# Squares summed over k by TensorE from pairs, modulation chunks in runs of four behind each quarter's first part, gate bursts of two, one and two

## The chip, the cores and the metric

The kernel runs on one core of a Trainium2 chip. The metric is the time of one execution on the device in microseconds (us). The engines are TensorE (PE), VectorE (DVE), ScalarE (ACT), GpSimd (POOL) and SyncE (SP); SP issues nearly all transfers, and its instructions, like those of every engine, run in the order in which they are written.

## The reference

One layer of a hybrid diffusion backbone is applied to 128 context tokens and 512 latent tokens with 2,048 channels, all in fp32. What matters here is its beginning:

```python
shift, scale, gate = jnp.split(mod, 3, axis=-1)   # mod = silu(c) @ w_ada + b_ada, once for c_ctx and once for c
h = rms_norm(x, norm_w)                            # x * rsqrt(mean(x*x) + EPS) * norm_w
h = h * (1.0 + scale[:, None, :]) + shift[:, None, :]
proj = h @ w_in                                    # 2048 -> 9216: nine parts of eight heads
...
out = jnp.concatenate([o_r, o_h], axis=-1).astype(x.dtype) @ w_out
x = x + (gate[:, None, :] * out).astype(x.dtype)
```

Between `proj` and `out` stand multi-scale retention and the HGRN2 recurrence, per head and in both directions. The final normalisation follows.

## The kernel before

**Tiles.** x lies transposed, as 16 tiles of 128 channels by 640 tokens (`x_in[:, k, :]`, k from 0 to 15; the first 128 columns are context tokens, the other 512 latent). A projection product takes fp32 operands that were split into a high and a low part in a reduced format (`w_hi`, `w_lo`, `hT_hi`, `hT_lo`) and computes hi*hi, hi*lo and lo*hi, each over two halves of 320 tokens: six products for each k. A chunk of w_in is 128 x 1024 values, eight k of 128 output columns; 18 chunks make a head. ACT writes `w_hi`, DVE writes `w_lo` (`split`), in two buffers, from three landing buffers (`raw`).

**Start.** Four loads bring x. ACT squares the 16 tiles into a ring of four buffers (`x_squares`, which borrows the place of the constants from column NSTART on). DVE adds them one after another into `var`. After the first modulation chunk PE multiplies `var` with a matrix of ones, which sums over the partitions (two products, L1726 and L1727), DVE and ACT make the reciprocal root, and DVE goes on with the modulation.

**Quarters.** The modulation vector is a product of `cs` (the two silu vectors) and w_ada. It is loaded in chunks of 1,024 KB (`load_ada`, tile `ada_raw`, four slots; `in_w_mod` chunks 0 to 31, then five of `in_w_first`); PE takes each with 16 fp32 products of 32 output rows (`ada_chunk`). Four chunks are a group; groups 0 to 3 give the scale of a quarter of the channels (four k). Behind a group PE transposes its row (`modulation_columns`), DVE scales x by it (L1096), ACT writes `hT_hi`, DVE `hT_lo` (L1102). Then `ahead(s)` can use these four k: for six slices of head 0, three "ahead" parts s of 24 products for each quarter. The loop over `group` from 1 to 4 is written out in the order below; PE runs it in just this order. A chunk's slot is free when PE has used it, and only then SP issues the load four chunks on. Into SP's list of modulation loads are put the first 12 w_in chunks and, at chunk 12, three small loads.

```python
ahead(s0)
ada_chunk(c0)
ada_chunk(c0 + 1)
ahead(s0 + 1, range(0, 2))
ada_chunk(c0 + 2)
ada_chunk(c0 + 3)
ahead(s0 + 1, range(2, 3))
modulation_columns(group)
ahead(s0 + 1, range(3, 4))
ahead(s0 + 2)
```

**Head 0 behind it.** Chunks 6 to 9 take the other modulation chunks between their products, and at the end five correction chunks (`correction`), which account for the shift. Chunks 10 to 17 are token chunks: five tiles of 128 tokens, each with six products of 512 columns. Between these tiles PE multiplies the gate's weights: 32 pieces of 512 KB (`gate_half`, `in_w_gate`, four slots, which are two of the modulation's slots), GATE_EACH of them behind tile number `at` in the chunk's order. `load_gate` waits until PE has used the piece four before. SP's `items(n, ...)` of head 0 hold, in order, the constants (n = 7), gate loads (n = 11 on), the retention states (n = 6) and eight copies that swap rows of the rotated keys and queries (n = 12, `swapped`), each from a wait of its own; w_in chunks from 12 on are loaded in between. Heads 1 to 7 follow, then the output projection.

## Time and profile before

| | |
|---|---|
| median of 3 runs | 1,489.37 us (1,489.04 to 1,490.95) |
| profiled execution, its time | 1,491.68 us |
| profiled execution, its span | 1,489.9 us |
| PE busy | 1,436.9 us, 96% of the span |
| DVE, ACT, POOL busy | 60%, 33%, 25% |
| chain that ended last: PE | 90% |
| chain that ended last: DMA, DVE | 4%, 3% |

The table is to be read with care at one place: a share over the whole span hides stages with different limits. PE's idle time is what the chain can lose, and the rows below show where it lies, by stage.

### The profile page before, as it was taken

The page shows a single profiled execution, that of the slowest core. Times are in us where ns is not written, and L with a number is a line of the kernel's source. Part 1 is how long each engine was busy: PE and PEld are TensorE (multiplying, and loading weights), DVE is VectorE, ACT ScalarE, POOL GpSimd, SP SyncE. Part 2 cuts the span into 40 slices and gives each one's busy share as a digit, 9 for nine tenths or more (in the row PEclk, how much of TensorE's full clock was granted, in tenths as well). Part 3 has the DMA queues.
Part 4 walks back from the last instruction along what each step waited for, and adds up shares of the span by engine and source line. Part 5 has one row for each costly group of instructions (what it writes and reads, how often), then busy time and mean ns, then how long its engine had stood idle before and what let it go on. Part 6 is the DMA issues. An engine that isn't in the chain of part 4 may idle for free.

```text
span 1489.9 us, 28075 instructions
## 1 busy us (share of the span) xinstructions
PE 1436.9 (96%) x11678; PEld 1278.6 (86%) x11678; DVE 889.0 (60%) x1208; ACT 493.5 (33%) x851; POOL 373.6 (25%) x292
## 2 busy tenths in 40 slices
PE   2999899999999999999999999999999999999996
PEld 2899569988998899889988998999899988788884
DVE  6634766565666665666576556666675658632346
ACT  4222334333333333333323332333243234321234
POOL 0000011532052216221621261135114415301220
PEclk9999999999999999999999999999999999999998
DMA  9789972322231223222313131322223237264236
GB/s 379 279 324 394 333 263 95 107 72 87 70 107 58 93 75 96 75 89 65 107 61 106 47 121 47 106 84 85 91 78 92 73 130 246 75 214 149 85 116 223
DMA packets 68763, 201.01 MB, mean 135 GB/s; under 512 B 8224, under 2 KB 16672, under 8 KB 62768
## 3 DMA queue, kind: packets, MB, share of 16 engines
q1 hardware_dynamic: 68656, 199.38, 38.7%
q8 instruction: 92, 1.51, 0.4%
q14 instruction: 15, 0.12, 0.0%
HBM read 178.62 MB, written 16.53 MB: 131 GB/s over the span
## 4 chain that ended last, share of the span: by engine, by line
PE 90%; DMA 4%; DVE 3%; SPq 1%; ACT 1%; POOL 0%; issue 0%; DVEq 0%; ACTq 0%
PE ps L1801 35%; PE ps L1830 10%; PE ps L1832 9%; PE ps L1831 9%; PE ps L2010 4%; PE ps L2012 4%; PE ps L2011 4%; PE ps L1853 2%; DMA area<-in_w_mod 2%; PE ps L1696 2%; PE ps L1717 2%; DMA area<-in_w_gate 1%; PE ps L1781 1%; PE ps L1866 1%; DVE area L1096 1%; DMA area<-in_w_out 1%
## 5 line engine op out<-in xcount | busy, mean ns | idle before, releaser
L1055 DVE TENSOR_TENSOR w_lo<-area,w_hi 128x1024 fp32r<-128x1024 f32 x144 | 184.4, 1280 | 374.7 <-ACT w_hi L621 374.2
L621 ACT ACTIVATE w_hi<-area 128x1024 fp32r<-128x1024 f32 x144 | 152.4, 1059 | 565.2 <-PE ps L1832 270.7
L1801 PE MATMUL ps<-hT_hi,w_hi 128*128 128x320 f32 x1184 | 276.8, 315 | 0.0
L1801 PE MATMUL ps<-hT_lo,w_hi 128*128 128x320 f32 x1184 | 269.7, 309 | 0.0
L1801 PE MATMUL ps<-hT_hi,w_lo 128*128 128x320 f32 x1184 | 269.7, 309 | 0.0
L1830 PE MATMUL ps<-w_hi,hT_hi 128*128 128x512 f32 x640 | 255.0, 398 | 0.0
L1832 PE MATMUL ps<-w_hi,hT_lo 128*128 128x512 f32 x640 | 249.6, 390 | 0.0
L1831 PE MATMUL ps<-w_lo,hT_hi 128*128 128x512 f32 x640 | 249.4, 390 | 0.0
L1801 PEld LDWEIGHTS ps<-hT_hi,w_hi 128*128 128x128 f32 x1184 | 195.7, 188 | 3.7 <-issue 1.4
L1801 PEld LDWEIGHTS ps<-hT_lo,w_hi 128*128 128x128 f32 x1184 | 198.0, 188 | 0.0
L1801 PEld LDWEIGHTS ps<-hT_hi,w_lo 128*128 128x128 f32 x1184 | 197.9, 188 | 0.0
L1830 PEld LDWEIGHTS ps<-w_hi,hT_hi 128*128 128x128 f32 x640 | 120.2, 188 | 28.5 <-issue 4.7
L1832 PEld LDWEIGHTS ps<-w_hi,hT_lo 128*128 128x128 f32 x640 | 120.1, 188 | 25.7
L1831 PEld LDWEIGHTS ps<-w_lo,hT_hi 128*128 128x128 f32 x640 | 120.3, 188 | 23.4
L1158 DVE RECIPROCAL area<-area 128x320 f32<-128x320 f32 x64 | 134.5, 2131 | 1.3
L2010 PE MATMUL ps<-w_hi,hT_hi 128*128 128x512 f32 x320 | 126.5, 395 | 2.2 <-DVE w_lo L1439 2.0
L2012 PE MATMUL ps<-w_hi,hT_lo 128*128 128x512 f32 x320 | 124.7, 390 | 0.0
L2011 PE MATMUL ps<-w_lo,hT_hi 128*128 128x512 f32 x320 | 124.7, 390 | 0.0
L1439 DVE TENSOR_TENSOR w_lo<-area,w_hi 128x1024 fp32r<-128x1024 f32 x40 | 53.2, 1330 | 111.9 <-ACT w_hi L899 111.9
L1617 POOL TENSOR_TENSOR area<-area 128x320 f32<-128x320 f32 x56 | 80.4, 1436 | 156.6 <-ACT area L746 156.6
L1606 POOL TENSOR_TENSOR area<-area 128x320 f32<-128x320 f32 x56 | 41.5, 741 | 301.6 <-PE ps L1853 244.8
L746 ACT ACTIVATE area<-area 128x1280 f32<-128x1280 f32 x56 | 71.3, 1273 | 122.1 <-DVE area L1254 117.4
(248 smaller groups left out, 1898.7 us busy)
## 6 DMA issues: line engine op xcount, KB each, us to landing
area<-in_w_in SPq DMA_DIRECT2D x144, 512.0 KB, 3.5
area<-in_w_mod SPq DMA_DIRECT2D x32, 1024.0 KB, 8.9
area<-in_w_out SPq DMA_DIRECT2D x40, 512.0 KB, 3.7
area<-in_w_gate SPq DMA_DIRECT2D x32, 512.0 KB, 5.8
area<-in_x_columns SPq DMA_DIRECT2D x4, 1280.0 KB, 9.9
area<-in_w_first SPq DMA_DIRECT2D x5, 1024.0 KB, 7.8
o_hi_scratch<-area SPq DMA_DIRECT2D x14, 320.0 KB, 2.2
o_lo_scratch<-area SPq DMA_DIRECT2D x14, 320.0 KB, 2.6
```

The lines of the kernel that those rows point to most:

```text
L621: act.activation(w_hi[:, n % 2, :], raw[:, n % 3, :], ACT.Copy).then_inc(wt_hi.sem, 1)
L746: act.activation(x, x, ACT.Exp).then_inc(xe.sem, 1)
L1055: v.tensor_tensor(w_lo[:, n % 2, :], raw[:, n % 3, :], w_hi[:, n % 2, :].bitcast(F32), ALU.subtract).then_inc(wt_lo.sem, 1)
L1158: v.reciprocal(part, part).then_inc(signal.sem, 1)
L1617: g.tensor_tensor(x[:, :, left], x[:, :, left], kf[:, :, left], ALU.mult)
L1801: ins = mm(out[s], wt[:, n % 2, w], x[:, k, s * HALF:(s + 1) * HALF], start=k == 0 and step == 0, stop=k == KT - 1 and step == 2)
L1830: mm(out, hT_hi[:, k, tile_cols(t)], w_hi[:, n % 2, w], start=k == 0, stop=False)
L1831: mm(out, hT_hi[:, k, tile_cols(t)], w_lo[:, n % 2, w], start=False, stop=False)
L1832: i = mm(out, hT_lo[:, k, tile_cols(t)], w_hi[:, n % 2, w], start=False, stop=k == KT - 1)
L2010: mm(out, hT_hi[:, k, tile_cols(t)], w_hi[:, m % 2, w], start=k == 0, stop=False)
L2011: mm(out, hT_hi[:, k, tile_cols(t)], w_lo[:, m % 2, w], start=False, stop=False)
L2012: return mm(out, hT_lo[:, k, tile_cols(t)], w_hi[:, m % 2, w], start=False, stop=k == KT - 1)
```

## The change

Four things are changed. (1) DVE adds the squares only in pairs, in place, and PE sums the eight pairs into two banks with eight pairs of products, ahead of the first modulation chunk; ACT waits for `x_total` before it writes a buffer again. (2) In the quarters the four modulation chunks of a group follow each other behind `ahead(s0)`; in the first group one chunk stands behind each of the first two k. The transposition comes behind the first k of the next part. Split 2 moves behind its quarter's last k. (3) The constants are loaded behind modulation chunk 16. (4) The gate pieces are taken two, one and two behind tiles 0, 2 and 4 of a token chunk (before: two behind tile 1, three behind tile 4), and their loads are written behind the other items of SP, up to three pieces further.

```diff
-GATE_FIRST, GATE_EACH = 10, (2, 3)
+GATE_FIRST, GATE_EACH = 10, (2, 0, 1, 0, 2)
...
             def items(n, h, prev):
-                if n == UNITS + 1 and prev is None:
-                    sp.wait_ge(x_sum.sem, x_sum.at(KT - 2))
-                    sp.dma_start(con[:, NSTART:NCONST], consts[:, NSTART:NCONST]).then_inc(con_in.sem, 16)
-                if prev is None and n > GATE_FIRST:
-                    for k in range(GATE_SLOTS, 6) if n == 11 else range(5 * n - 54, min(5 * n - 49, GATE_HALVES)):
-                        load_gate(k)
...
+            def gate_loads(n):
+
+                for k in range(max(5 * n - 51, GATE_SLOTS), min(5 * n - 46, GATE_HALVES)) if n > GATE_FIRST else range(0):
+                    load_gate(k)
+
             def head(h, prev):
                 for n in range(CHUNKS):
                     if not first_head(h) or n >= 12:
                         load(h, n)
                     items(n, h, prev)
+                    if prev is None:
+                        gate_loads(n)
...
+                if c_ == 16:
+                    sp.wait_ge(x_total.sem, x_total.at(KT // 2 - 1))
+                    sp.dma_start(con[:, NSTART:NCONST], consts[:, NSTART:NCONST]).then_inc(con_in.sem, 16)
...
-                if k >= SQUARES:
-                    act.wait_ge(x_sum.sem, x_sum.at(max(k - SQUARES - 1, 0)))
+                if k >= SQUARES and k % 2 == 0:
+                    act.wait_ge(x_total.sem, x_total.at((k - SQUARES) // 2))
                 act.activation(x_squares[:, k % SQUARES, :], x_in[:, k, :], ACT.Square).then_inc(x_sq.sem, 1)
...
-            for k in range(1, KT):
-                dve.wait_ge(x_sq.sem, x_sq.at(k))
-                if k > 1:
-                    dve.wait_ge(x_sum.sem, x_sum.at(k - 2))
-                v.tensor_tensor(var, x_squares[:, 0, :] if k == 1 else var, x_squares[:, k % SQUARES, :], ALU.add).then_inc(x_sum.sem, 1)
+            for j in range(KT // 2):
+                one, two = (x_squares[:, (2 * j + i) % SQUARES, :] for i in range(2))
+                dve.wait_ge(x_sq.sem, x_sq.at(2 * j + 1))
+                v.tensor_tensor(one, one, two, ALU.add).then_inc(x_sum.sem, 1)
...
+            for j in range(KT // 2):
+                pair = x_squares[:, 2 * j % SQUARES, :]
+                pe.wait_ge(x_sum.sem, x_sum.at(j))
+                mm(ps[:, A, :], ones, pair[:, P:T], start=j == 0, stop=j == KT // 2 - 1)
+                mm(ps[:, BB, 0:P], ones, pair[:, 0:P], start=j == 0, stop=j == KT // 2 - 1).then_inc(x_total.sem, 1)
...
             for group in range(1, QUARTERS + 1):
                 c0, s0 = group * GROUP_CHUNKS, (group - 1) * AHEAD
...
+                if group == 1:
+                    for k in range(ADA_K):
+                        ahead(s0, range(k, k + 1))
+                        if k < 2:
+                            ada_chunk(c0 + k)
+                else:
+                    ahead(s0)
+                for c_ in range(c0 + 2 if group == 1 else c0, c0 + GROUP_CHUNKS):
+                    ada_chunk(c_)
+                ahead(s0 + 1, range(0, 1))
                 modulation_columns(group)
-                ahead(s0 + 1, range(3, 4))
+                ahead(s0 + 1, range(1, 4))
                 ahead(s0 + 2)
```

**PE in the first token chunk, chunk 10.** Before: the products of the second tile (the last three of them), the five small correction transposes (L1761), the first two gate pieces (L1781), the third tile.

```order
L1830 MATMUL ps<-w_hi,hT_hi 128x512
L1831 MATMUL ps<-w_lo,hT_hi 128x512
L1832 MATMUL ps<-w_hi,hT_lo 128x512
L1761 MATMUL ps<-con,area 128x32 [waits corr_rows]
L1761 MATMUL ps<-con,area 128x32 x4
L1781 MATMUL ps<-area 32x256 [waits g_landed0]
L1781 MATMUL ps<-area 32x256 x3
L1781 MATMUL ps<-area 32x256 [waits g_landed1]
L1781 MATMUL ps<-area 32x256 x3
L1830 MATMUL ps<-w_hi,hT_hi 128x512 [waits corr_rows]
```

Of the change, from the end of the first tile (L1786 are the gate pieces, L1766 the transposes):

```order
L1835 MATMUL ps<-w_hi,hT_hi 128x512
L1836 MATMUL ps<-w_lo,hT_hi 128x512
L1837 MATMUL ps<-w_hi,hT_lo 128x512
L1786 MATMUL ps<-area 32x256 [waits g_landed0]
L1786 MATMUL ps<-area 32x256 x3
L1786 MATMUL ps<-area 32x256 [waits g_landed1]
L1786 MATMUL ps<-area 32x256 x3
L1835 MATMUL ps<-w_hi,hT_hi 128x512
L1836 MATMUL ps<-w_lo,hT_hi 128x512
L1837 MATMUL ps<-w_hi,hT_lo 128x512
```

The first two pieces have moved ahead of one tile, and the transposes now stand one tile behind them.

**SP at the gate loads.** Before, behind the last correction chunks (L404); L508 are small bias rows, L456 the retention states, L440 the constants, L473 the swaps:

```order
L412 DMA area<-in_w_gate 128x1024 [waits a_used] x4
L508 DMA area<-in_b_ada 2x512 [waits g_clear]
L508 DMA area<-in_b_ada 2x512 x3
L456 DMA area<-in_state_ret_fwd 128x128 [waits h_lo]
L456 DMA area<-in_state_ret_bwd 128x128
L440 DMA con<-in_constants 128x2688 [waits x_sum]
L412 DMA area<-in_w_gate 128x1024 [waits g_used] x2
L429 DMA area<-in_w_in 128x1024 [waits wt_lo]
L412 DMA area<-in_w_gate 128x1024 [waits g_used] x5
L473 DMA area<-area 32x512 [waits r_fixed]
L473 DMA area<-area 32x512 x7
L429 DMA area<-in_w_in 128x1024 [waits wt_lo]
```

Of the change (L450 the states, L467 the swaps):

```order
L450 DMA area<-in_state_ret_fwd 128x128 [waits h_lo]
L450 DMA area<-in_state_ret_bwd 128x128
L412 DMA area<-in_w_gate 128x1024 [waits g_used] x5
L429 DMA area<-in_w_in 128x1024 [waits wt_lo]
L467 DMA area<-area 32x512 [waits r_fixed]
L467 DMA area<-area 32x512 x7
L412 DMA area<-in_w_gate 128x1024 [waits g_used] x5
L429 DMA area<-in_w_in 128x1024 [waits wt_lo]
```

The constants are gone from here, five gate loads now stand ahead of the w_in load and of the swaps, and the next five stand behind the swaps.

**ACT at the squares.** Before, the second four squares wait once each for the running sum:

```order
L611 ACTIVATE con<-area 128x640 [waits x_landed0] x4
L611 ACTIVATE con<-area 128x640 [waits x_sum,x_landed1] x4
L611 ACTIVATE con<-area 128x640 [waits x_sum,x_landed2] x4
L611 ACTIVATE con<-area 128x640 [waits x_sum,x_landed3] x4
L621 ACTIVATE w_hi<-area 128x1024 [waits landed0]
```

Of the change:

```order
L615 ACTIVATE con<-area 128x640 [waits x_landed0] x4
L615 ACTIVATE con<-area 128x640 [waits x_total,x_landed1]
L615 ACTIVATE con<-area 128x640 [waits x_landed1]
L615 ACTIVATE con<-area 128x640 [waits x_total,x_landed1]
L615 ACTIVATE con<-area 128x640 [waits x_landed1]
L615 ACTIVATE con<-area 128x640 [waits x_total,x_landed2]
```

Every second square now waits for a product of PE instead of an addition of DVE.

## Rows read from the trace of the kernel before

**Rows 1.** Busy time by stage: window, us, each engine, granted clock, DMA, GB/s.

```profile
0.00:35.61 35.61, 8.33 (x134) 5.93 (x134) 22.48 (x40) 15.87 (x23) 0.73 (x5) 0.98 0.94 379
35.61:101.62 66.01, 62.96 (x806) 58.61 (x807) 35.00 (x68) 16.82 (x21) 0.00 (x0) 0.96 0.78 310
101.62:148.15 46.53, 45.94 (x741) 42.53 (x739) 16.47 (x43) 9.84 (x16) 0.00 (x0) 1.00 0.92 368
148.15:215.68 67.53, 61.70 (x449) 41.81 (x446) 47.02 (x69) 22.76 (x36) 5.08 (x4) 1.00 0.88 316
215.68:1489.90 1274.22, 1257.95 (x9560) 1129.68 (x9558) 768.05 (x989) 428.20 (x755) 367.83 (x283) 1.00 0.31 101
```

**Rows 2.** Timeline of the start: start us, duration us, engine, instruction, idle before.

```profile
7.79 2.61 ACT L611 ACTIVATE con<-area 128x640 f32<-128x640 f32 x4 [4.51 <-DMA area<-in_x_columns]
9.19 0.82 DVE L1050 TENSOR_TENSOR area<-con 128x640 f32<-128x640 f32 x1 [4.78 <-ACT con L611]
...
17.55 2.62 ACT L611 ACTIVATE con<-area 128x640 f32<-128x640 f32 x4 [0.48 <-DMA area<-in_x_columns]
...
23.29 2.08 PE L1726 MATMUL ps<-area,con 128*128 128x512 f32 x2
...
25.16 0.64 PE L1727 MATMUL ps<-area,con 128*128 128x128 f32 x2
...
25.83 0.69 DVE L1060 TENSOR_SCALAR area<-ps 128x512 f32<-128x512 f32 x1 [1.67 <-PE ps L1727]
...
31.47 0.29 DVE L1076 COPY area<-ps 128x128 f32<-128x128 f32 x1
```

**Rows 3.** Timeline of PE, two fp32 products of head 0's successor.

```profile
246.53 0.38 PE L1877 MATMUL ps<-area 128*128 128x128 f32 x2
246.75 0.39 PE L1878 MATMUL ps<-area 128*128 128x128 f32 x2
```

**Rows 4.** Chain of work that ended last, 35 to 102 us: start, duration, what.

```profile
35.61 6.12 PE ps L1717 x24
...
58.44 1.88 PE ps L1696 x64
...
65.77 13.57 DMA area<-in_w_mod
...
97.22 4.40 PE ps L1717 x30
```

**Rows 5.** Waits, 0 to 350 us: total us, times, longest.

```profile
PE ps L1717 <- DVE hT_lo L1102: 6.0, 4, 3.5
```

**Rows 6.** Timeline of PE at the second quarter's products.

```profile
56.40 0.57 PE L1717 MATMUL ps<-hT_hi,w_hi 128*128 128x320 f32 x2 [1.60 <-DVE hT_lo L1102]
```

**Rows 7.** Busy time by window: three short stretches.

```profile
34.00:35.00 1.00, 0.00 (x0) 0.00 (x0) 1.00 (x3) 0.81 (x2) 0.00 (x0) 0.50 1.00 418
56.00:60.00 4.00, 3.60 (x72) 3.41 (x76) 1.54 (x3) 1.44 (x2) 0.00 (x0) 1.00 0.01 2
65.00:68.00 3.00, 3.00 (x23) 3.00 (x22) 2.54 (x9) 0.84 (x2) 0.00 (x0) 1.00 0.15 50
```

**Rows 8.** Timeline of PE at gate pieces of the first token chunks.

```profile
161.19 0.64 PE L1781 MATMUL ps<-area 128*32 128x256 f32 x8 [2.57 <-DMA area<-in_w_gate]
...
164.70 1.12 PE L1781 MATMUL ps<-area 128*32 128x256 f32 x16
...
170.06 1.50 PE L1781 MATMUL ps<-area 128*32 128x256 f32 x24
171.50 0.50 PE L1830 MATMUL ps<-w_hi,hT_hi 128*128 128x512 f32 x1
```

**Rows 9.** Timeline of PE's weight loads at the second gate piece.

```profile
152.67 0.16 PEld L1781 LDWEIGHTS ps<-area 128*32 128x32 f32 x8 [0.38 <-DMA area<-in_w_gate]
```

**Rows 10.** Timeline of SP's issues at the constants and the swaps.

```profile
150.26 0.56 SPq L440 DMA_DIRECT2D con<-in_constants  x1
...
166.26 5.07 SPq L473 DMA_DIRECT2D area<-area  x8
```

29 lines of the change are left out of this document (8 added, 21 removed).

## The prediction

> **What bounds the kernel now.** I read first the busy time by stage [rows 1]. TensorE (PE) is busy for 1,257.95 of the last 1,274.22 us, and the change touches nothing there. What it can win lies before 215.68 us: PE idles 27.3 us until the first projection product at 35.61, 3.05 us in the four quarters until 101.62, 0.59 us until 148.15, and 5.83 us in the six token chunks until 215.68, 36.8 us together. The DMA share beside it is 0.94, 0.78, 0.92 and 0.88, so that the transfers are nearly as tight as PE: a PE wait that goes away may come back at the next transfer. Then I read each stage's own limit.
>
> Start: the squares of x on ScalarE (ACT) follow four loads of x, which come 3.25 us apart (7.79 to 17.55), VectorE (DVE) adds one tile after another from 9.19 to 23.0, two fp32 products on PE give the sum at 25.80, and the DVE chain of the variance, Newton step and first modulation copy begins at 25.83 and reaches the copy at 31.47 [rows 2]. The reader is to see that 5.64 us distance; the change does not touch it. Quarters: the chain runs through PE, through the DVE conversions behind each modulation, and through one transfer, the modulation chunk that is issued at 65.77 and lands 13.57 us later [rows 4]; PE waits for the conversions four times, 6.0 us in all, of which 3.5 is the first [rows 5] and the longest other 1.6 [rows 6]. Of the 3.05 us the three later ones are 2.5, which leaves 0.5 for the wait for that chunk. Token chunks: three waits for gate pieces, 2.57 us in the first chunk; they sum to the 5.83 us of that stage [rows 1, 8].
>
> **The squares.** Fifteen adds become eight, and one pair of products becomes eight pairs. DVE loses 7 x 0.85 us, which was on the path, but ACT now waits, before every second square from the fifth on, until PE has summed the pair whose buffers it overwrites: two pairs in flight. One turn of that ring is ACT 1.4 us for two squares (2.61 for four, and the end of the second), DVE 0.85, and PE. At the lower clock level PE needs 2.5 us for a pair (23.29 to 25.80 [rows 2]); at the higher, 128-column fp32 products start 0.22 us apart [rows 3], so 640 columns take 1.1 us and the result 0.2 more. The turn is 1.4 + 0.85 + 1.3 and three hand-overs of 0.04, 3.65 us for two pairs. The first pair is ready at 9.19 + 0.85 = 10.0 and summed at 12.6. PE starts slow: 24 products from 35.61 took 6.12 us where 30 took 4.40 later [rows 4], so the higher rate came some 5 us after PE began; the granted clock there is 0.50, the lower level of 1.2 GHz [rows 7]. Counted from 10.0 this is 15. The odd pairs are then summed at about 14.6, 18.3, 21.9 and 25.6, the even ones earlier. If the rate rises at 13.5 the last is at 25.4, at 17 it is 26.2. I take 25.8, as before: the term is 0, bounds -0.4 and +0.4. The serial adds have been exchanged for a ring with the same end. The cover of the four modulation chunks that now come behind the sums is the DVE chain: they take 3.8 us (two take 1.88 [rows 4]) where 5.64 is free; without it they would stand on the path with 3.8.
>
> The Trainium skill (TensorE: Matmul & The Clock Gate, the HAM clock gate) says that an array that has been idle starts at its lower rate and that sustained work releases it. By that rule alone the gaps in the new ring could keep it low; the rows do not show products with such gaps, and the rival for it is below.
>
> **The quarters.** A product takes 4.40/30 = 0.147 us, a modulation chunk 0.94, a switch between the two kinds 0.1. In the first group one chunk stands behind each of the first two k, which costs two switches (0.2) and brings the group's transposition from 48.4 to about 46.8: twelve products (1.76) now stand behind it instead of before it. In each later group the run of four saves two switches. Behind the transposition PE has 42 products, 6.17 us, instead of 30, 4.40. The 1.77 us more cover the longest of the three later waits for conversions, 1.6, in which split 2 stood, and so all 2.5 us of them go [rows 5, 6]; if that cover were gone, they would be back. Split 2, moved behind the quarter's last k, is done some 4 us before its product.
>
> What comes late next is the transfer. Group 2's chunks run from 56.6, so the load for group 3's first chunk is issued at 57.6; it was 59.5, behind the chunk at 58.44 [rows 4]. The DMA queue is empty before (0.01 busy from 56 to 60) and crawls behind the three small loads (0.15 busy from 65 to 68 [rows 7]); both move along with it. The fourth chunk then lands at 79.34 - 1.9 = 77.4. Between the third's landing and it stand a w_in and itself, 512 and 1,024 KB, 3.8 us at the 418 GB/s of [rows 7], so the third lands at 73.6. PE starts the run of four at 71.1 and wants the third at 73.0 and the fourth 0.94 us behind it. Waits: 0.6 + 2.9 = 3.5 us, where 0.5 was. The constants (1,344 KB, 3.3 us at the same rate) are now queued behind chunk 16: group 4's last chunk lands at 92.1 and is wanted at about 92.1; a wait of up to 1 us is possible, and without the constants there would be 3 us to spare. The group ends are: transposition at 46.8, 61.3, 79.4 and 94.0, then 6.17 us, 100.2 against 101.62. The term is -1.3 us. Bounds: -4.1 if the transfers do not bind, +1 if they bind 2 us later than I count. From there to 148.15 every load waits for a slot that PE frees, so the shift carries through.
>
> **The gate stage**, in times of before. Two things are cheap to see. The constants no longer stand at 150.26 in SP's queue [rows 10] in front of pieces 4 and 5, which land 3.3 us earlier; the 2.57 us wait goes. The bursts are three per chunk: one piece takes 0.64 us and three 1.50 [rows 8], so 0.43 each and 0.21 for the burst, and the product around it starts 0.1 late on both sides (0.50 against 0.39 at 171.50). A third burst costs 0.4 us, six times: +2.4 us. Then the order. Piece 0 and 1 are wanted behind the first tile (some 1.4 us, from 161.8 to 164.7 for two [rows 8]), at 149.6 and 150.1; the second landed at 152.67, when PE had waited for it by 0.38 [rows 9]. SP issues them when the correction chunks free their slots, as before, so PE waits 2.6 us here, 2.2 more than before. Pieces 2 to 8 are in time. Piece 9 is not: SP issues it behind the eight row swaps, 5.07 us of issue [rows 10], which wait for the bias correction on ACT, itself 3.6 us late because the correction transposes now stand behind the late pieces. Issued at 168.5, landing some 4.5 later, wanted at 171: 2 us. The pieces behind it catch up, since each is now asked for as soon as its slot is free, four tiles ahead of its use. The next w_in is now issued behind the five gate loads; it lands 5.6 us into the chunk before it and it is split at about 8 of 10.1, so 2 us are left. Sum: -5.83 + 2.2 + 2.0 + 2.4 = +0.8 us. Bounds: -3.4 (no wait left, only bursts) and +3.5 (the w_in margin of 2 us used up once as well).
>
> **Sum.** 0 - 1.3 + 0.8 = -0.5 us. The profiled execution took 1,491.68 us with a span of 1,489.9; by it the changed kernel is at 1,491.2. The median of the runs is 2.3 us below it, so the time I give is 1,489.37 - 0.5 = 1,488.9 us.
>
> **Rivals.** (1) The transfers give way: the fourth chunk of group 3 lands as early as PE wants it, and pieces 0, 1 and 9 as well. For it speaks that the DMA share is only 0.78 in the quarters; against it the 13.57 us landing, in which the queue was full but for the small loads. Terms: 0, -4.1 and -3.4, or half of both if they give way in part: 1,481.9 to 1,485.6 us. It decides from 2.5 us less waiting than I count. Chance 0.22. (2) The clock stays at its higher level in the gap before 35.61, because PE has now worked since 10. Then the first quarter's 24 products cost 3.5 instead of 6.1 us: 1,488.9 - 2.6 = 1,486.3. Against it: the gap is as long as before, and before it the level was lost. Chance 0.06. (3) Slower: the ring never reaches the higher level. PE then needs 2.5 us a pair, eight in a row end at 30.0 instead of 25.8, the variance chain and with it everything to 35.61 is 4.2 us late: 1,493.1 us. It decides from 3.5 us of delay, six pairs at the lower level. Against it: at the lower level PE has no gap at all in the ring, since 2.5 x 2 exceeds the other parts, and without gaps it did rise. Chance 0.07. (4) Slower in the token chunks: the w_in that is now issued behind five gate loads is late in several chunks, and SP stands behind the swaps longer than I count. Two chunks late by 2 us give 1,492.9 us; it decides from 3.5 us. Chance 0.10. (5) The three parts cancel as forecast, within 3 us: chance 0.55.
>
> **How the numbers follow.** A measurement of this kernel tells about 0.2%, 3.0 us, from no change. Faster: rival 1 and a third of rival 2, 0.24. Slower: rivals 3 and 4, 0.17, of which some would stay within the bound but the forecast case's upper tail makes up for it. Same: 0.59. The forecast case's own range is 1,486.5 to 1,491.5. The range to be held 8 times in 10 reaches into rivals 1, 3 and 4: 1,485.2 to 1,492.2.
>
> **What would show it.** Right: the variance read on DVE near 25.8; eight pairs of products from 10 on, the first two about 2.5 us and the last about 1.3; no wait for hT_lo after the first; a PE wait of 2 to 4 us for a modulation chunk near 77; a wait for the second gate piece behind the first tile, one near the end of the second token chunk, none for pieces 4, 11 and 21; token chunks of 10.1 instead of 9.7 us. Wrong: the variance read before 24.5 or after 28; the four-chunk run of group 3 without a gap; w_lo as the releaser of a token chunk.

## The result, and the profile after

The changed kernel takes 1,493.45 us (median of 10 runs, 1,491.53 to 1,496.49) where the kernel before, beside it, takes 1,489.72 (10 runs, 1,488.80 to 1,491.37). The ratio is 1.0024, 95% interval 1.0014 to 1.0034: 3.7 us slower, between 2.1 and 5.1. The forecast was 0.5 us faster, 1,488.9, and its upper end 1,492.2. The two profiled spans are 1,492.1 and 1,489.9, so a single pair of profiles holds 2.2 us of the loss; the other 1.5 us is the place of the two profiled executions among their runs, 0.4 us above the median here and 2.0 above it before.

Busy time by stage of the changed kernel, cut where [rows 1] is cut (first product of the quarters, first slice of chunk 6, first token product, first product behind the retention scores):

```profile
0.00:35.54 35.54, 17.14 (x161) 10.08 (x162) 16.79 (x33) 16.20 (x23) 0.73 (x5) 0.96 0.94 381
35.54:100.85 65.31, 62.52 (x806) 59.00 (x807) 35.11 (x68) 16.86 (x21) 0.00 (x0) 0.94 0.83 332
100.85:149.21 48.36, 46.23 (x740) 42.64 (x739) 16.47 (x43) 9.92 (x17) 0.00 (x0) 0.99 0.92 363
149.21:217.58 68.37, 65.14 (x450) 41.62 (x446) 47.92 (x69) 23.75 (x37) 5.57 (x4) 0.98 0.82 294
217.58:1492.10 1274.52, 1258.30 (x9560) 1129.56 (x9558) 769.04 (x990) 427.28 (x754) 367.92 (x283) 1.00 0.30 101
```

Against [rows 1] the stages differ by -0.07, -0.70, +1.83, +0.84 and +0.30 us. The reader is to see the granted clock too: 0.94, 0.99 and 0.98 where 0.96, 1.00 and 1.00 stood. In the token stage PE idles only 3.2 us instead of 5.8 and yet the stage is longer: it is busy 3.4 us more with the same products. Two causes can be told apart over all twenty profiles. In the six with the old bursts and no stretch at the lower level in this stage (before, e2, e4, g4, h3 and h4 below) PE is busy for 61.6 to 61.8 us, and in the six such ones with the new bursts (f1, f2, f3, g2, h2, i2) for 63.7 to 64.2: the third burst costs 2.3 us of PE in the mean. The rest is the 2.7 us of this stage that ran at the lower level.

The start, DVE and PE in the timeline (columns as in [rows 2]):

```profile
24.37 1.13 PE L1727 MATMUL ps<-con 128*128 128x512 f32 x2 [0.49 <-DVE con L1052]
25.33 0.38 PE L1728 MATMUL ps<-con 128*128 128x128 f32 x2
...
25.75 0.69 DVE L1062 TENSOR_SCALAR area<-ps 128x512 f32<-128x512 f32 x1
...
31.40 0.29 DVE L1078 COPY area<-ps 128x128 f32<-128x128 f32 x1
```

The variance is read at 25.75 (25.8 forecast, 25.83 before [rows 2]), and the ring's last pair takes 1.3 us. That part went as forecast.

Group 3 of the quarters and the last correction chunk, PE in the timeline:

```profile
70.56 3.14 PE L1697 MATMUL ps<-area 128*32 128x128 f32 x96
76.38 1.53 PE L1697 MATMUL ps<-area 128*32 128x128 f32 x32 [2.68 <-DMA area<-in_w_mod]
77.84 0.90 PE L1718 MATMUL ps<-hT_hi,w_hi 128*128 128x320 f32 x2
78.54 0.74 PE L1718 MATMUL ps<-hT_lo,w_hi 128*128 128x320 f32 x2
...
80.33 0.46 PE L1718 MATMUL ps<-hT_lo,w_hi 128*128 128x320 f32 x2
...
147.90 1.38 PE L1759 MATMUL ps<-area 128*32 128x128 f32 x32 [2.12 <-DMA area<-in_w_first]
149.21 0.80 PE L1835 MATMUL ps<-w_hi,hT_hi 128*128 128x512 f32 x1
149.80 0.63 PE L1836 MATMUL ps<-w_lo,hT_hi 128*128 128x512 f32 x1
```

and the windows behind them (columns as in [rows 7]):

```profile
74.00:76.50 2.50, 0.12 (x4) 0.12 (x8) 0.00 (x0) 0.00 (x0) 0.00 (x0) 1.00 1.01 427
76.50:80.50 4.00, 4.00 (x43) 3.58 (x41) 0.69 (x5) 0.00 (x0) 0.00 (x0) 0.57 1.01 425
147.00:151.00 4.00, 3.10 (x36) 2.42 (x37) 1.66 (x3) 1.65 (x2) 0.00 (x0) 0.69 0.82 291
```

PE waits for the fourth chunk, as forecast (2.68 us; 2.9 was counted). The price is larger than the wait: behind it the granted clock is at the lower level (1.2 GHz) from 76.9 to 80.3, and two products of 320 columns take 0.74 us instead of 0.46. The same stands behind the wait of 2.12 us at the last correction chunk, from 148.5 to 152.0.

The end of the token stage, PE, DVE and SP:

```profile
172.63 0.64 PE L1786 MATMUL ps<-area 128*32 128x256 f32 x8 [1.24 <-DMA area<-in_w_gate]
...
195.90 8.27 SPq L412 DMA_DIRECT2D area<-in_w_gate  x5
204.21 0.43 SPq L429 DMA_DIRECT2D area<-in_w_in  x1
...
211.86 1.23 DVE L1057 TENSOR_TENSOR w_lo<-area,w_hi 128x1024 fp32r<-128x1024 f32 x1 [2.87 <-ACT w_hi L625]
213.00 1.94 DVE L1125 SCALAR_TENSOR_TENSOR area<-hT_hi,area,hT_lo 128x128 f32<-128x128 f32 x4
214.85 1.71 DVE L1132 TENSOR_TENSOR hT_lo<-area,hT_hi 128x640 fp32r<-128x640 f32 x2
216.49 0.68 DVE L1401 TENSOR_TENSOR area<-ps,area 128x512 f32<-128x512 f32 x1
...
217.22 0.49 PE L1996 MATMUL ps<-area 128*128 128x128 f32 x2 [1.93 <-DVE area L1401]
```

The same split on DVE in the kernel before:

```profile
206.79 1.23 DVE L1055 TENSOR_TENSOR w_lo<-area,w_hi 128x1024 fp32r<-128x1024 f32 x1 [4.95 <-ACT w_hi L621]
```

The wait of 1.93 us at 217.22 is new. SP issues a w_in only behind five gate loads, the last of which waits for a slot; so the split of that w_in comes on DVE at 211.86 instead of 206.79 (that DVE idles ahead of it is no sign, it did so before as well), and the third DVE step behind it makes the masked scores that PE wants. The prediction had looked for w_lo itself as the releaser; the late w_in shows three instructions further on.

### The profile page after: what moved, and what is told of

It reads as the page before. It is cut to its first block, busy times and chain, and to the rows that moved or that the text cites. A ratio compares the mean times of both kernels' runs of the same rounds, so it can differ in the third digit from the quotient of the medians.

```text
span 1492.1 us, 28104 instructions
## 1 busy us (share of the span) xinstructions
PE 1449.3 (97%) x11706; PEld 1282.9 (86%) x11706; DVE 885.3 (59%) x1201; ACT 494.0 (33%) x851; POOL 374.2 (25%) x292
## 4 chain that ended last, share of the span: by engine, by line
PE 91%; DMA 3%; DVE 2%; ACT 1%; SPq 1%; issue 1%; POOL 0%; DVEq 0%; ACTq 0%
PE ps L1806 35%; PE ps L1835 10%; PE ps L1837 9%; PE ps L1836 9%; PE ps L2015 4%; PE ps L2016 4%; PE ps L2017 4%; PE ps L1718 2%; PE ps L1858 2%; PE ps L1697 2%; DMA area<-in_w_mod 1%; PE ps L1871 1%; PE ps L1786 1%; PE ps L1882 0%; PE ps L1911 0%
## 5 line engine op out<-in xcount | busy, mean ns | idle before, releaser
L1618 POOL TENSOR_TENSOR area<-area 128x320 f32<-128x320 f32 x56 | 80.4, 1436 | 156.6 <-ACT area L749 156.6
```

Source lines behind the costliest of these rows:

```text
L1618: g.tensor_tensor(x[:, :, left], x[:, :, left], kf[:, :, left], ALU.mult)
```

## The experiments

Each is compared with runs of the kernel before on the same chip; 0.001 is 1.5 us. The e, f, g runs and the h and i runs were on four different chips, so the times of kernels of different letters are set against each other by their ratios. The letters e to i stand for rounds: e is the kernel before with one edit, f the changed kernel with one edit, and what g, h and i start from is said with them. Token stage is the time from the first token product to the first product behind the retention scores, in the one profile of each. The place where the first one starts is given because it matters below.

| kernel | ratio [95%] | first token product | token stage |
| --- | --- | --- | --- |
| before | 1 | 148.15 | 67.53 |
| changed | 1.0024 [1.0014, 1.0034] | 149.21 | 68.37 |
| e1 squares alone | 1.0010 [0.9998, 1.0022] | 148.47 | 67.13 |
| e2 runs of four alone | 0.9997 [0.9986, 1.0008] | 147.43 | 66.10 |
| e3 gate part alone | 1.0013 [1.0003, 1.0022] | 146.16 | 70.20 |
| e4 constants alone | 0.9986 [0.9973, 0.9999] | 148.41 | 64.75 |
| f1 three pairs | 1.0019 [1.0010, 1.0028] | 147.23 | 67.31 |
| f2 w_in ahead | 1.0011 [1.0001, 1.0021] | 148.63 | 68.47 |
| f3 both waits filled | 1.0007 [0.9998, 1.0016] | 148.39 | 68.05 |
| f4 old gate part | 1.0005 [0.9995, 1.0015] | 147.25 | 67.56 |
| g1 before, three edits | 0.9997 [0.9988, 1.0006] | 147.66 | 66.53 |
| g2 products at the start too | 1.0003 [0.9993, 1.0013] | 147.90 | 67.39 |
| g3 small loads late | 1.0020 [1.0009, 1.0031] | 149.43 | 68.50 |
| g4 candidate | 0.9976 [0.9965, 0.9987] | 147.15 | 66.18 |
| h1 one wait filled | 1.0000 [0.9991, 1.0009] | 148.77 | 67.72 |
| h2 g4, new gate part | 1.0007 [0.9998, 1.0017] | 145.75 | 70.55 |
| h3 g4, old squares | 0.9982 [0.9972, 0.9991] | 145.57 | 66.23 |
| h4 waits filled, old gates | 0.9989 [0.9979, 0.9998] | 147.25 | 65.01 |
| i1 bursts, w_in ahead | 0.9997 [0.9988, 1.0006] | 145.43 | 71.34 |
| i2 bursts alone | 0.9982 [0.9973, 0.9991] | 146.25 | 67.20 |

**The parts alone (e1 to e4).** Each takes one part of the diff into the kernel before. The line that marks each part:

```diff
e1 +                v.tensor_tensor(one, one, two, ALU.add).then_inc(x_sum.sem, 1)
e2 +                ahead(s0 + 1, range(0, 1))
e3 +GATE_FIRST, GATE_EACH = 10, (2, 0, 1, 0, 2)
e4 +                if c_ == 16:
```

In e1 the constants stay at their old place; in e4 they wait for the old sum.

> Before, with the pair sums of the squares on TensorE alone. Theory A (ring of two pairs): the variance is read within 0.4 us of the 25.83 us of before, and the time stays within 0.5 us of before. Theory B (TensorE's clock: because it works from 10 us on, its level is lost at other places later): the variance is at the same place, but a stretch of half clock appears behind a wait, and the time is 1.5 to 3 us above before.

> Before, with the modulation chunks in runs of four and split 2 at its quarter's end alone. Theory A: the first chunk products of head 0 start at 100.2 to 100.9 instead of 101.62, with a wait of 2 to 3 us for the last chunk of the third run and a stretch of half clock behind that wait (it costs some 1.6 us); time -1.3 to 0 us against before. Theory B: the wait is there but no half clock behind it, since the early work of TensorE is missing; time -2.5 us or less.

> Before, with the gate bursts of two, one and two and their loads behind SP's other items alone (the constants stay where they were). Theory A: token chunks of 10.1 us without a wait, a wait of 2 us behind the first tile, one for the ninth piece or so, and a wait of 1 to 2 us of TensorE for the retention scores on VectorE in the sixth token chunk, because w_in is issued behind five gate loads; time +2 to +4 us against before. Theory B: these waits only stand in for those that go; time within 1 us of before.

> Before, with the constants loaded behind modulation chunk 16 alone. Theory A: the 2.57 us wait for gate piece 4 goes, and no chunk of the fourth modulation group is late (0 to 0.5 us); time -2.5 us against before. Theory B: the wait goes but the next pieces bring it back, time within 1 us of before.

Squares +1.5, runs -0.4, gates +1.9, constants -2.1 us by the ratios; the sum is +0.9 with a joint half-width of at least 3.4 us (root of the sum of squares of 1.8, 1.6, 1.4 and 1.9, and all four share one set of runs of the kernel before), and the whole is +3.6. So the parts don't contradict the whole and don't explain it. In e1 the level rose at 13.0 us instead of 15.4, and the variance was read at 25.05. One theory fell at once: that the lower clock behind the fourth chunk comes from PE's new early work. The runs of four alone, with the old squares, wait 2.69 us at 76.53 and have the lower level from 77.0 to 80.4.

**A third pair of buffers for the squares (f1).** The pair borrows two tiles that are free until the sum is read.

```diff
-                if k >= SQUARES and k % 2 == 0:
-                    act.wait_ge(x_total.sem, x_total.at((k - SQUARES) // 2))
+                if k >= 6 and k % 2 == 0:
+                    act.wait_ge(x_total.sem, x_total.at((k - 6) // 2))
```

> The changed kernel with one more pair of buffers for the squares of x (three pairs in flight instead of two; the other two buffers are rstd and newt, which are free until the sum is read). In the changed kernel ACT waited about 0.5 us for PE before every second square, a turn of the ring took 3.72 us, and the variance was read at 25.75. If the ring of two pairs is what keeps the start at its old length: ACT waits for PE no more after the first pairs, the last pair is summed 1.1 to 1.3 us behind the last square, the variance is read at 23.0 to 23.8, and the first product comes at 33.5 to 34.0 instead of 35.54, since the fourth modulation chunk lands at 28.5 whatever the squares do. The time is then 1,491.7 (1.8 us below the changed kernel) if nothing later eats it. Rival: the start is held by the modulation chunks or by the lower clock level on PE, and the first product stays at 35.2 to 35.6: 1,493.4.

Timeline of this kernel, DVE and PE:

```profile
22.55 0.69 DVE L1066 TENSOR_SCALAR area<-ps 128x512 f32<-128x512 f32 x1
...
29.70 1.08 PE L1701 MATMUL ps<-area 128*32 128x128 f32 x32 [2.09 <-DMA area<-in_w_mod]
...
30.92 0.29 DVE L1082 COPY area<-ps 128x128 f32<-128x128 f32 x1 [2.76 <-PE ps L1701]
```

The ring was the limit of the sum (3.2 us earlier), but not of the start: the copy comes 0.5 us earlier, since the fourth modulation chunk lands at 29.6. First product at 35.20. The rival was nearer: here a sum that is ready 3.2 us earlier buys 0.3 us, and not even that lasts. The lower level stood for 10.2 us (31.1 to 41.3) where the changed kernel has 6.8 (32.5 to 39.3), and the first transposition of the quarters came at 46.87 instead of 46.19.

**The order of loads in the gate part (f2).** The gate loads of a chunk are issued behind the next w_in.

```diff
                     if not first_head(h) or n >= 12:
                         load(h, n)
+                    if prev is None:
+                        gate_loads(n)
                     items(n, h, prev)
-                    if prev is None:
-                        gate_loads(n)
```

In gate_loads the set moves along by one chunk: 5 * n - 56 for 5 * n - 51, from n = 12 on.

> The changed kernel, with the five gate loads of a chunk issued behind the load of the next w_in instead of ahead of it. Theory: the wait of 1.93 us at 217.22 (retention scores behind DVE L1401) comes from the w_in that was issued behind five gate loads, landed at 210.78 (205.70 before) and made ACT and DVE split it 5 us later. Then that w_in lands near 206, DVE L1401 is done near 212, and the wait is gone: 1.9 us less behind 205, 1,491.5. The wait for the chunk at 147.9 (2.1 us) and the half clock behind it are untouched and should stand as they were, as should the 2.7 us at 76.4. Rival: the late split does not set that wait (the swaps of the rotation or the bias correction do), and it stays at 1.5 to 2.0 us with the w_in landing early: 1,493.4.

The wait at 217 is gone, as in theory, but pieces now come late instead: 1.66 us at 152.77 and 2.37 at 174.06 (1.24 before this edit). The token stage is 68.47 against 68.37. A mechanism shown, and no gain: the wait has moved.

**Products in the waits (f3, h1).** PE multiplies something nobody reads while it would wait; h1 has the first of the two places only.

```diff
+                    if group == 3 and c_ == c0 + 3:
+                        pe.wait_ge(mod_steps.sem, mod_steps.at(0, mods_known(2)))
+                        filler(ada_bank(4), 0, 17)
                     ada_chunk(c_)
...
+                    filler(DD, KT - 1, 14)
                     correction(CORRECTIONS - 1)
```

> The changed kernel with products added whose sums nobody reads: 17 products of 320 columns (2.5 us at the higher level) in front of the fourth modulation chunk of group 3, where PE waited 2.68 us until 79.0, and 14 (2.1 us) in front of the last correction chunk, where it waited 2.12 us until 147.9. Both into a bank that is free there. Theory: behind each of the two waits PE ran at half clock for 3.4 us (76.9 to 80.3 and 148.6 to 152.0), which cost 1.7 us each; with the products PE is not idle, the clock stays up at both places, group 3 ends 1.5 us earlier, and at the second place up to 1.7 us come back less what the gate pieces, which landed at 152.0, then make PE wait: 2 us less in all, 1,491.5. Rival 1: the clock level was worth nothing since the transfers set the pace: the levels stay up but later waits grow by what is won, 1,493.4. Rival 2: the half clock does not come from the idle time and stands in spite of the products: 1,493.4 to 1,494.

> The changed kernel with only the 17 products (320 columns) ahead of the fourth modulation chunk of group 3. With both waits filled the time was 1,491.99 against 1,490.69, 1.3 us above before. Theory: the half clock of 3.4 us behind this chunk, which stood in three of three profiles of kernels with this gate-independent part unchanged, is the systematic part of the loss; the later wait in front of the last correction chunk differs by 1 to 2 us from execution to execution of one and the same code (first token chunk at 149.21, 148.63, 147.25). Then this kernel is 1.3 to 1.9 us faster than the changed one: 1,491.3 to 1,492.2 with before at 1,490.7. Rival: the half clock there is given back by group 4's chunks, which the transfers bind, and the time is that of the changed kernel, 1,493.4 to 1,494.

Timeline of f3 on PE, and its clock in the window that was at 0.57:

```profile
74.42 2.76 PE L1703 MATMUL ps<-hT_hi 128*128 128x320 f32 x17
77.23 1.08 PE L1697 MATMUL ps<-area 128*32 128x128 f32 x32
```

```profile
76.50:80.50 4.00, 3.95 (x52) 3.48 (x51) 1.20 (x7) 0.00 (x0) 0.00 (x0) 1.00 1.03 434
```

The level stays up at both places in f3 and at the first in h1. A profile is one execution, but the mean granted clock is on record for each: 0.9934 in the mean of the ten of the changed kernel, 0.9930 in f2, 0.9942 in f3 and in h1. So the lower level follows the idle time. 0.0008 of 1,490 us is 1.2 us of PE. The ratios fall by 0.0017 and 0.0024, 2.5 and 3.6 us, each give or take 2. In h1's profile the transposition of group 3 is at 78.67 instead of 79.61 and that of group 4 at 93.70 instead of 94.42; this shows under 1 us of it, and its second wait (2.48 us at 147.53) still has the lower level behind it. That filling helps is shown; that it is worth more than the 1.7 us which 3.4 us at half clock can cost isn't. The kernel before has 0.9936 to 0.9941 in its five sets of runs, so over all executions the lower level accounts for about 0.3 to 1.0 us of the loss. The one pair of profiles (0.9948 before and 0.9924 changed, 3.6 us) overstates it.

**The old gate part in the changed kernel (f4).**

```diff
-GATE_FIRST, GATE_EACH = 10, (2, 0, 1, 0, 2)
+GATE_FIRST, GATE_EACH = 10, (2, 3)
...
+                    for k in range(GATE_SLOTS, 6) if n == 11 else range(5 * n - 54, min(5 * n - 49, GATE_HALVES)):
```

> The changed kernel with the gate part of the kernel before (bursts of two and three, its order of loads), so squares, runs of four and the constants behind chunk 16 are left of the change. The gate part alone cost 1.7 us against before (1,492.30 against 1,490.58). Theory: the gate order accounts for its share here too, above all the w_in behind five gate loads and the pieces wanted behind the first tile: the wait at 217.2 goes, pieces 0 and 1 are not wanted before the second tile, third bursts (2.4 us) are gone: 1,490.5 to 1,491.5. The rest of the loss, the wait in front of the last correction chunk (1.85 us with the constants moved alone, 2.12 in the changed kernel, 0.59 before), stays at 1.7 to 2.2 us. Rival: the parts add up as measured alone, squares +1.4, runs -0.1, constants -1.9: 1,490.0 with a wait there of 0.5.

1.0005: the gate part is 2.8 us of the 3.6, give or take 2.1. Its last correction chunk waited 0.41 us and not 2. So that wait is no property of the change: this kernel, the changed one and f2 have the same instructions up to the first token product, and it stands at 147.25, 149.21 and 148.63. The kernel before and e3 are also the same up to there: 148.15 and 146.16. Some of this may lie between chips; f2 and f4 ran on one and are 1.4 us apart.

**The start and the small loads (g1 to g4).** Eight products of ones by ones ahead of the first transposition and 14 behind it; the three small loads behind chunk 24 instead of 12. g1 is the kernel before with the constants moved, these products (7 and 14) and 8 ahead of the last correction chunk; g2 is f3 with them; g3 is the changed kernel with the loads moved alone; g4 is f4 with both and the 8 products. Nobody reads the added sums.

```diff
+            start_filler(8)
             modulation_columns(0)
+            start_filler(14)
...
-                if c_ == 12:
+                if c_ == 24:
                     sp.dma_start(lgr, ret_decay.rearrange("l s h -> l (s h)").broadcast_to([P, 2 * HEADS])).then_inc(small_in.sem, 16)
```

> A candidate, built from the kernel before: the constants moved behind modulation chunk 16 (alone: 1,488.66 against 1,490.58), 7 products of ones by ones (0.22 us each) in front of the first transposition and 14 behind it, in PE's idle time of 1.76 and 3.46 us, and 8 products of 320 columns (1.2 us) in front of the last correction chunk, where that kernel waited 1.85 us. Nobody reads the added sums. Theory: with no idle stretch of 3 us PE's clock does not fall at 34, the first quarter's 24 products take 3.5 us instead of 6.1, and this lasts to the end: 1,488.7 - 2.3 = 1,486.4 us. Rival: the level is lost in spite of the products, or the 2.3 us are given back where a modulation chunk lands late: 1,488.7.

> The changed kernel with the products of the run before last (17 ahead of the fourth modulation chunk of group 3, 14 ahead of the last correction chunk) and, as well, 8 products of ones by ones in front of the first transposition and 14 behind it, where PE was idle for 2.1 and 3.5 us. Theory: the clock keeps its higher level from 14 on without a fall at 32.5, the first products (24, 6.1 us) take 3.5 us, the transposition of group 1 comes at 43.9 instead of 46.2, and 2.3 us less stand at the end if the transfers let them: 1,491.99 - 2.3 = 1,489.7. Rival: the higher level comes, but the fourth chunk of group 3 is issued earlier only by what PE gained and the waits behind it grow, since the queue is full there: half is given back, 1,490.8 to 1,492.

> The changed kernel with its three small loads (decay, norm weight, bounds) issued behind modulation chunk 24 instead of 12. Theory: the 2.7 us for which PE waited at 76.4 for the fourth chunk of group 3 came from the stretch at 65 to 68 us in which the queue crawled behind these loads (0.15 busy). Without them the chunk lands at 76.4 less about 2, PE waits under 1 us, no half clock follows (it took 3.4 us and cost 1.7), and group 3 ends 3.5 us earlier: 1,490.0 us. Rival: the transfers of group 3 are late for another reason (the load is issued when its slot is freed, 57 to 62, and the bytes ahead of it take their time): the wait stays at 2 us or more, and the time at 1,493. A second place to watch is behind chunk 24, where the same stretch would now stand.

> A candidate, built from the changed kernel with the gate part of before (1,491.93 us): the three small loads behind chunk 24, 8 and 14 products of ones by ones around the first transposition, and 8 products of 320 columns ahead of the last correction chunk. If both theories hold (the small loads delay the fourth chunk of group 3, the idle time costs the clock), no half clock stands anywhere before the token chunks, group 3's wait is under 1 us, and the time is 1,491.9 - 2.3 - 3.4 = 1,486.2. If only the clock at the start is won: 1,489.6. Rival: transfers give it all back: 1,491.9.

Transpositions of the four groups in the PE timelines, us:

| kernel | 1 | 2 | 3 | 4 |
| --- | --- | --- | --- | --- |
| before | 48.37 | 65.08 | 81.38 | 96.95 |
| changed | 46.19 | 60.68 | 79.61 | 94.42 |
| f3 | 46.76 | 61.25 | 79.22 | 93.75 |
| g2 | 44.79 | 59.28 | 77.51 | 93.36 |
| g3 | 46.37 | 60.87 | 75.53 | 91.97 |
| g4 | 44.55 | 59.05 | 73.57 | 91.59 |

Against f3, g2 wins 1.97 us at the start (2.3 expected): the clock does not fall before the first products. At the fourth group 0.39 is left, because the last chunk lands late:

```profile
91.36 1.08 PE L1697 MATMUL ps<-area 128*32 128x128 f32 x32 [1.14 <-DMA area<-in_w_mod]
```

In g3 the crawl behind the small loads is gone, and with it the wait and the lower level at 76. The window is that of [rows 7]:

```profile
65.00:68.00 3.00, 3.00 (x22) 3.00 (x21) 2.93 (x6) 1.73 (x3) 0.00 (x0) 1.00 0.99 416
```

Group 3 is 4.1 us earlier, group 4 only 2.45 (a wait of 1.38 us at 89.97); behind chunk 24, where the small loads now stand, PE waits 2.25 us, and 2.65 at the last correction chunk. Time 1.0020: the gain was real where it was made, and the later waits took it back. g1 is no faster than the kernel before, though its mean granted clock is 0.9961 for 0.9941 (3.0 us of PE): the higher level alone bought it no time. g4 keeps its lead through the gate stage, by the old gate part, and is faster than the kernel before: 1,487.83 us against 1,490.84, 0.9976, with the changed kernel at 1.0024. The constants alone (e4) had 0.9986, so how much of this the other edits give, 1.5 us give or take 2.5, isn't told apart from nothing.

g4 was expected to have no stretch at half clock before the token chunks. It has one, and it prices such a stretch. g4 and h3 (below, the same quarters) reach the third transposition at 73.57 and 73.56 and wait 1.37 and 1.36 us for the fourth chunk of group 4. In g4 the level fell (88.6 to 92.0), in h3 it didn't, and the fourth transposition comes at 91.59 and 90.23: the fall cost 1.4 us, the same wait. PE of g4, then of h3:

```profile
88.24 1.65 PE L1693 MATMUL ps<-area 128*32 128x128 f32 x32 [1.37 <-DMA area<-in_w_mod]
89.82 0.90 PE L1722 MATMUL ps<-hT_hi,w_hi 128*128 128x320 f32 x2
```

```profile
88.23 1.08 PE L1694 MATMUL ps<-area 128*32 128x128 f32 x32 [1.36 <-DMA area<-in_w_mod]
89.24 0.56 PE L1723 MATMUL ps<-hT_hi,w_hi 128*128 128x320 f32 x2
```

**What g4's parts are worth (h2 to h4).** Each replaces one part of g4:

```diff
h2 +GATE_FIRST, GATE_EACH = 10, (2, 0, 1, 0, 2)
h3 +            for k in range(1, KT):
h4 +                        filler(ada_bank(4), 0, 17)
h4 +                if c_ == 12:
```

h2 has the new gate part, h3 the old squares, and h4 products in the wait of group 3 in place of the moved small loads.

> The best kernel so far (0.9976 of before) with the change's gate part in place of the old one: bursts of two, one and two, and its order of loads. Theory: the gate part costs by itself what it cost alone (1.7 us, interval 0.4 to 3.3), through the third burst in each of six chunks (2.4 us) and the wait of 1.3 to 1.9 us at 215 to 217 for the scores behind the late w_in, less the waits for pieces that go: 1,487.8 + 1.7 to 3.0 = 1,489.5 to 1,490.8. Rival: the loss measured alone was the other parts' clock and landings, and with these mended the new gate part is as good as the old: 1,487.8.

> The best kernel so far with the squares of before: serial adds on VectorE and one pair of products, ahead of the second modulation chunk. Theory, from the prediction: the ring of two pairs ends where the serial adds did (variance read at 25.8 both), so nothing is lost or won, 1,487.8; and with the added products in the gap PE's clock is up before the first products of a quarter in either. Rival: the squares part alone measured 1.4 us slower than before (interval -0.3 to 3.3), and undoing it here wins that: 1,486.4.

> The changed kernel with the old gate part and added products at the three idle places (8 and 14 around the first transposition, 17 ahead of the fourth chunk of group 3, 8 ahead of the last correction chunk), but with the small loads left where they are. It differs from the best kernel in how group 3 is mended: products in the wait there, loads out of the way here. Theory: what made the best one fast is that the chunk lands 2.5 us earlier, since products only keep the clock and still wait; group 3 ends at about 77.5 and group 4 is then bound by its own chunks, 1,489.5 to 1,490.5. Rival: the clock was all that mattered: 1,487.8.

The new gate part costs 0.0031, 4.6 us, give or take 2.2. In the profiles it even started 1.4 us earlier than g4 and was 3.0 later behind the scores, where the new wait is longest and a stretch at the lower level follows it. Timeline of h2, DVE and PE:

```profile
210.59 1.23 DVE L1057 TENSOR_TENSOR w_lo<-area,w_hi 128x1024 fp32r<-128x1024 f32 x1 [5.23 <-ACT w_hi L625]
...
215.95 0.49 PE L2007 MATMUL ps<-area 128*128 128x128 f32 x2 [2.90 <-DVE area L1401]
...
216.89 0.63 PE L1848 MATMUL ps<-w_hi,hT_lo 128*128 128x512 f32 x1
```

The same split in g4:

```profile
203.19 1.23 DVE L1053 TENSOR_TENSOR w_lo<-area,w_hi 128x1024 fp32r<-128x1024 f32 x1 [3.24 <-ACT w_hi L621]
```

Old squares: 0.9982 against 0.9976, no difference beyond the 2 us that these runs resolve, which fits the squares' term of zero. h4 is at 0.9989, 1.9 us above g4, give or take 2.2: it leans to the theory, that the chunk's landing counts and not its clock alone, and doesn't settle it.

**The gate part taken apart (i1, i2).** Both start from g4. i1 has the new bursts and the loads as in f2. i2 has the bursts alone, one line:

```diff
-GATE_FIRST, GATE_EACH = 10, (2, 3)
+GATE_FIRST, GATE_EACH = 10, (2, 0, 1, 0, 2)
```

> The best kernel with the new gate part (the run before, 1,491.73), but each w_in load issued ahead of the chunk's five gate loads. Theory: the 4 us by which the new gate part was slower there come mostly from the wait of 2.90 us at 216 for the scores and the half clock behind it (217.0 to 220.4, 1.7 us), both from the w_in that lands at 209.7 behind five gate loads (202.1 with the old order). With w_in ahead that wait is gone, waits of 1.5 to 2.4 us for pieces near 152 and 174 stay as in the changed kernel with w_in ahead, and the time is 1,491.7 - 3 = 1,488.5 to 1,489.5. Rival: the third burst and the pieces are the cost, and nothing is won: 1,491.5.

> The best kernel (1,487.8) with the bursts of two, one and two, and the old places of the gate loads. It measures the third burst: six chunks, 0.4 us each by the prediction's count, 2.4 us, less what the waits for pieces near 169, 175 and 206 (4.5 us together in the best kernel) lose, as the middle piece is asked for one tile earlier and the last two are as late as before. Theory: a wash or a cost under 1.5 us: 1,487.5 to 1,489.3, and no wait for the scores at 215. Rival: bursts cost the full 2.4 us: 1,490.2.

i2 is at 0.9982, 0.9 us above g4, give or take 2.1. The profiles show why it is so little. The token stage is 1.0 us longer (67.20 for 66.18): PE is busy for 63.7 us instead of 61.6, so the third burst's cost is there, and the gate waits sum to 3.5 us where g4 has 4.5. i1 was expected at 1,489 and is at 1,490.88. It has no wait for the scores; its price is one wait of 3.85 us for piece 9, issued behind the row swaps, and the lower level behind it. Timeline of i1:

```profile
171.50 1.08 PE L1796 MATMUL ps<-area 128*32 128x256 f32 x8 [3.85 <-DMA area<-in_w_gate]
172.51 0.79 PE L1846 MATMUL ps<-w_hi,hT_hi 128*128 128x512 f32 x1
```

So it is the order of the loads that costs, by whichever of the two waits: h2 is 3.7 us above i2, give or take 1.9, and i1 is 2.2 above it, give or take 1.9, all three with the same bursts.

## Why the prediction was wrong, by its own steps

The terms, in us, stand beside two readings of the profiles. "Pair" is the changed kernel less the kernel before. "Means" is the difference between the mean of several kernels with the new form of the stage and that of several with the old one, without those that have added products in it or the small loads moved (start: before, e2, e3, e4 against changed, e1, f2, f3, f4, h1; quarters and chunks 6 to 9: before, e1, e3, e4 against changed, e2, f1, f2, f4; token chunks: below).

| stage | forecast | pair | means |
| --- | --- | --- | --- |
| start | 0 | -0.07 | +0.2 |
| quarters | -1.3 | -0.70 | -0.2 |
| chunks 6 to 9 | 0 | +1.83 | +0.1 |
| token chunks | +0.8 | +0.84 | +1.7 |
| behind them | 0 | +0.30 | |

**Quarters: the step that failed.** The transpositions were put at 46.8, 61.3, 79.4 and 94.0, and stand at 46.19, 60.68, 79.61 and 94.42. The three later conversion waits went, and the waits for chunks were 2.68 us for the 3.5 counted. What failed is that a wait was counted as its own length: the granted clock behind it was put at nothing. Group 3 takes 18.93 us where groups 2 and 4 take 14.49 and 14.81; 2.68 of it is the wait, and 3.4 us at half clock cost up to 1.7. The same stands in the profiles of e2, f2 and f4. The mean granted clock of all their executions agrees: 0.9931, 0.9930 and 0.9924, where the kernel before has 0.9936, 0.9940 and 0.9940 in the same sets, 0.7 to 2.4 us of PE. Where the level fell behind one of two equal waits, the fall cost 1.4 us (g4 against h3). It need not fall. In the twenty profiles, between 45 and 235 us, it fell at 11 of the 17 waits of 2.0 to 3.9 us and kept up at 6 (the kernel before at 161.19, 2.57 us; f1 at 77.02, 2.63), and at 3 of the 51 waits of 1.0 to 2.0 us it fell. The second fault is the base. The forecast started from one execution that was late here: the four kernels with the old quarters start chunk 6 at 99.6 to 101.5 us, 100.5 in the mean, the kernel before at 101.5 as the last; the five with the new ones start it at 100.6. So the gain of 1.3 us that the forecast set against the gate part is 0.2 at most in these profiles (-0.4 us, give or take 1.6, by the timed runs of e2).

**Carry-through.** "The shift carries through" to 148.15 did not hold in the pair: 0.77 us ahead became 1.06 behind, with a wait of 2.12 us instead of 0.59 at the last correction chunk and the lower level behind it. That is scatter for the most part. f4 has the same instructions up to the first token product, starts chunk 6 within 0.1 us of the changed kernel and waits 0.41 us, and in the means the stage is equally long in both orders, 47.3 us. The start of the token stage scatters by 2 us between executions of identical instructions. This also bounds what one profile can say of a difference of 2 us; I had priced each stage to 0.1 us from one.

**Gate stage: the sum was near, its lines were not.** +0.8 was forecast and the pair of profiles has +0.84. The nearness is in part luck. In the mean of three kernels with the old gate part and the constants at their old place (before, e1, e2) the token stage takes 66.9 us, and in the nine with the new bursts, moved gate loads and early constants 68.6: +1.7. The paired runs hold the constants still. Without the 2.57 us that the forecast gave to the constants, it put the gate part at +3.4, and 1.9 (e3 against before), 2.8 (changed against f4) and 4.6 (h2 against g4) were measured. So these runs do not refute its size. Line by line:

- The 5.83 us of waits that were to go are those of one execution, the most of any with the old gate part. The nine profiles with the old gate part have 4.1 us in the mean, the ten with the new loads 4.0.
- Pieces 0 and 1 were to wait 2.6 us. In the changed kernel, which starts the stage late, they don't; i2 has 0.36 and 1.10. The 0.38 us that was taken off was idle time of the weight loads [rows 9] and no part of PE's 5.83, so that by its own rows the sum was +1.2.
- Piece 9 was to wait 2 us and waits 1.24, 0.85 to 3.85 in the ten. In the changed kernel pieces 4, 11 and 21 no longer wait; in four of the other nine piece 11 still does, 0.3 to 0.5 us.
- "It is split at about 8 of 10.1, so 2 us are left" is wrong. All eight kernels with the w_in behind five gate loads wait for the scores, 1.03 to 2.90 us, and none of the other twelve does. This is the mechanism of rival 4, which I had given 0.10, and it sits three DVE steps behind the w_in, where I had not looked.
- Six third bursts at 0.4 us, 2.4 us: right, 2.3 us of PE in the mean.
- 2.7 us of the stage ran at the lower level, 1.4 us that no line had.

**Start.** Right at every step. Rival 3 (the ring never reaches the higher level) did not come: the level rose at 15.4, where 15 was counted. The Trainium skill (TensorE: Matmul & The Clock Gate, the HAM clock gate) says that sustained work releases the array from its lower rate. The trace agrees: from 9.96 us to the rise PE had one idle stretch, of 0.24 us. The gaps of 0.5 us between pairs came behind the rise, from 16.9 on, and the level stayed up, so no run here shows whether work with such gaps lifts it. Rival 2, a level kept into the first products, needs work in the gap: with it, g2 wins 2.0 us where 2.6 were counted.

**What is still open.** The timed loss is 3.6 us, between 2.1 and 5.1. The stage means above add up to 1.8, and which stage has the rest isn't shown. The gate part costs between 1.9 and 4.6 by its three timed comparisons, each give or take about 2. The forecast had set more against it than came: -2.57 for the constants (-2.1 measured, give or take 1.9) and -1.3 for the quarters (-0.4, give or take 1.6). Why e4 alone measured 2.1 us faster when g1, with the same constants and added products, measured none, is below what these runs resolve.

## What to carry to other kernels

A PE wait of 2 to 3 us in a stage where the clock is up should be priced at its length plus nothing or 1.4 to 1.7 us, by whether the granted clock falls behind it (11 times of 17 here). To keep transfers from being late removed the wait itself (g3, group 3); throwaway products in the wait kept the clock but not the time of the wait, and the two did not differ clearly (g4 and h4, 1.9 us, give or take 2.2). When loads for two consumers share one queue in order, follow each consumer's load through to the engine that finally waits for it, several instructions behind the landing. A lead won early is not kept if later transfers are not asked for earlier as well: in g2 2 us became 0.4 within four groups. And before a wait of one profile is entered as a gain, look at the same wait in a second execution: here 5.8 us of waits in one profile were 4.1 in the mean of nine.

## Not expected of the hardware

Three small loads keep the whole queue nearly still for 3 us: 0.15 busy from 65 to 68 us [rows 7], 0.99 there with them moved. The last correction chunk's load was issued at 141.90 and its product started at 147.13 in the kernel before, 5.2 us behind it, and 6.8 us behind it (141.12, 147.90) in the changed one. Executions of identical instructions reach the first token product up to 2 us apart. Wherever the clock level fell later than 45 us it stood low for 3.4 us, behind waits of 1.4 to 2.9 us and behind two of 1.22 and 0.98 us close together (e3), and for 6.8 us at the wait of 3.85 us (170.9 to 177.7 in i1, from 0.6 us before its end on). Waits of the same length left it alone elsewhere.
